# Three operand buffers declared further down in on-chip memory

## The chip, the cores and the metric

The kernel runs on one NeuronCore of a Trainium2 chip. The metric is the device time of one execution in microseconds (us). A core has a matmul engine (TensorE, PE in the profile, its weight loads shown apart as PEld), a vector engine (VectorE, DVE), an activation engine (ScalarE, ACT), GpSimd (POOL) and a queue that issues the DMAs (SyncE, SP). They share an on-chip memory (SBUF) of 128 partitions. A buffer has the same byte offset in each partition.

## The reference

A model of width 1024 on 256 tokens. Two layers of a transformer-like block come first:

```python
for i in range(DEPTH):                      # DEPTH = 2
    h = rmsnorm(x, norm1_g[i])
    mix = hybrid_mixer(h, w_in[i], ...)     # three kinds of sparse attention, 16 heads
    x = x + mix @ w_out[i]
    h = rmsnorm(x, norm2_g[i])
    x = x + conv_glu_ffn(h, w_up[i], conv_w[i], conv_b[i], w_down[i])   # hidden width 2816
return rmsnorm(x, final_g)
```

A third layer follows, with four branches of width 256 (a linear recurrence, pooling, a gated chunked recurrence, a short convolution), which are projected to 1024, gated, summed and sent through `w_out`; then a feed-forward block with hidden width 4096 and a squared ReLU:

```python
merged = jnp.sum(gates * branch_out, axis=2)
h = h + rms_norm(jnp.einsum("btd,de->bte", merged, w_out[l]), norm_mix_post[l])
hid = jnp.square(jax.nn.relu(jnp.einsum("btd,df->btf", rms_norm(h, ...), w_up[l])))
h = h + rms_norm(jnp.einsum("btf,fd->btd", hid, w_down[l]), norm_mlp_post[l])
```

All is fp32.

## The kernel before

**Weights.** `stream_plan` lists about 170 tiles of 128 x 2048 fp32 values in the order of use. SyncE loads them into the four slots of `raw`. ScalarE rounds a tile to fp32r into `whi` (L1288); VectorE (L1744) or GpSimd (L2575) subtracts and stores the rest into `wlo`. Both have three slots.

**Activations** are split in the same way into a high and a low part: `hh` and `hl`, the halves of `hb2`, for the input of a projection, `gh` and `gl` for the hidden values of a feed-forward block. A product is the sum of three fp32r matmuls: high x high, high x low, low x high.

**`gh`, `gl`, `mg`** hold [128, 2, 2, 256] fp32r values each, 4096 bytes per partition. They serve four ends:
- the hidden values between `up` and `down`: ScalarE writes `gh` (L1421, and L1718 in the third layer), VectorE `gl` (L2105, L2540), PE reads both in `down` (L720 to L722) and `down_quarter` (L734 to L736);
- the first two blocks of the attention's output (`mixed_at`) before `w_out`, read at L577, L578 and L580;
- the output of a branch of the third layer, read at L1211 to L1213;
- the merged branches (`merged_at`), `gh`, `gl` and `mg` before `w_out` of the third layer.

In all of these matmuls the piece of `gh`, `gl` or `mg` is the first operand, the one that is loaded into the array (LDWEIGHTS, 128 x 128), and 512 columns of `whi` or `wlo` stream through:

```python
ah, al = gh[:, j % 2, k, s], gl[:, j % 2, k, s]
...
e.matmul(o, ah, wh[:, k, c], start=j == 0 and k == 0, stop=False)
e.matmul(o, ah, wl[:, k, c], start=False, stop=False)
mm = e.matmul(o, al, wh[:, k, c], start=False, stop=last and k == 1)
```

In the `up` matmuls (L697, L702, L703) it is the other way: a weight slot is loaded, and `hb2` streams, 512 columns (high and low) or 256.

**Order.** Each engine's program is written out by hand, with semaphores between them. No planner decides anything by a buffer's address.

**Where buffers lie.** `sb` allocates in the order of the calls. Each start is rounded up to 32 bytes, and `raw` starts at byte 16,512. So the starts before are, in bytes per partition:

| buffer | start | | buffer | start |
|---|---|---|---|---|
| raw | 16,512 | | PQ | 150,176 |
| whi | 49,280 | | gb | 193,696 |
| wlo | 73,856 | | rl | 197,792 |
| X | 98,432 | | E | 201,888 |
| XN | 106,624 | | PT | 210,080 |
| hb2 | 114,816 | | sm | 214,176 |
| gh | 131,200 | | sc | 218,784 |
| gl | 135,296 | | selm | 220,832 |
| mg | 139,392 | | vbd | 221,856 |
| prmt | 143,488 | | cc | 223,136 |
| mskt | 147,872 | | th, lv | 225,184, 227,232 |

`prmt` has 4376 bytes, which isn't a multiple of 32. The buffers up to it start at multiples of 64, those behind it 32 bytes past a multiple of 64.

Of the kernel before, what the change touches and what calls it, by code (L numbers as in the profile page):

```python
# [8 lines left out]
F32R = mybir.dt.float32r  # L9
# [6 lines left out]
L = 256  # L16
# [128 lines left out]
def program(nc, wst, prm, msk, prm2, gains, lvl, x, out):  # L145
    ctx = ExitStack()
    with ctx:
        def sb(name, shape, dt=F32):
            return ctx.enter_context(nc.sbuf_tensor(name, shape, dt))
# [14 lines left out]
        XN = sb("XN", [128, 2, D])  # L164
        hb2 = sb("hb2", [128, 8, 2, L], F32R)
        hh, hl = hb2[:, :, 0, :], hb2[:, :, 1, :]
        gh = sb("gh", [128, 2, 2, L], F32R)
        gl = sb("gl", [128, 2, 2, L], F32R)
        mg = sb("mg", [128, 2, 2, L], F32R)
        prmt = sb("prmt", [128, NPRM])  # L170
        mskt = sb("mskt", [128, 9, 128], BF16)
        PQ = sb("PQ", [128, 2 * PCOLS + 22 * L])
# [7 lines left out]
        sc = sb("sc", [128, 2, L])  # L180
        selm = sb("selm", [128, 2, L], BF16)
        vbd = sb("vbd", [80, 5, 64])
        cc = sb("cc", [128, 2, L])
        th = sb("th", [128, 2, L])
        lv = sb("lv", [128, 8, 128], mybir.dt.uint16)
# [2665 lines left out]
```

How the kernel before makes its waits and increments, by code:

```python
    def wait_ge(self, sem, value):  # L129
        if self.seen.get(sem.name, 0) < value:
            self.e.wait_ge(sem, value)
            self.seen[sem.name] = value
# [374 lines left out]
        def rope(e, q, room, step, done, c0, nh, hd, r2, cos, sin):  # L507
            n = 2 * nh * r2
            view = P[:, :, c0:c0 + nh * hd].rearrange("p t (h d) -> p t h d", d=hd)
            x1, x2 = view[:, :, :, 0:r2], view[:, :, :, r2:2 * r2]
            tb = [w[:, 0:n].rearrange("p (t h r) -> p t h r", t=2, r=r2) for w in room]
            def tab(name):
                return par(name).rearrange("p (t r) -> p t r", t=2).unsqueeze(2).broadcast_to([128, 2, nh, r2])
            e.tensor_tensor(tb[0], x1, tab(cos), ALU.mult)
            e.tensor_tensor(tb[1], x2, tab(sin), ALU.mult)
            e.tensor_tensor(tb[2], x2, tab(cos), ALU.mult)
            e.tensor_tensor(tb[3], x1, tab(sin), ALU.mult).then_inc(*step())
            q.wait_ge(*q.prev)
            e.tensor_tensor(x1, tb[0], tb[1], ALU.subtract)
            e.tensor_tensor(x2, tb[2], tb[3], ALU.add).then_inc(*done)
# [6 lines left out]
            def bank_free(b):  # L529
                if free[b] is not None:
                    q.wait_ge(*free[b])
# [1 line left out]
            def weights_ready(m):  # L533
                q.wait_ge(*hi[m])
                q.wait_ge(*lo_of(m)[m])
# [1 line left out]
            def keep_warm(n, bank):  # L537
                q.wait_ge(*dve["warm"])
                bank_free(bank)
                for i in range(n):
```

## Time and profile before

| | |
|---|---|
| runs of the kernel before | 1032.85, 1035.64, 1035.68 us (median 1035.64) |
| the profiled execution's own time | 1032.85 us |
| its span, first to last instruction | 1031.5 us |
| PE busy | 1021.9 us, 99% |
| PE weight loads | 858.8 us, 83% |
| VectorE, ScalarE, GpSimd busy | 765.6, 551.4, 224.8 us |
| mean granted TensorE clock | 1.000 |
| DMA | 179.16 MB, 174 GB/s |

The profile is of one execution. Weight loads overlap the matmuls before them. Busy time of an engine is the union of its instructions; a wait is idle time of an engine, put down to what ended it. "Chain" is the sequence of work that ended last, followed backwards from the last instruction.

### The profile page before, as it was taken

To read this page: it belongs to the slowest core of one execution; us is meant where nothing else is said; L and a number is where in the kernel's file an instruction comes from. 1 tells how busy PE (TensorE), PEld (TensorE's weight loads), DVE (VectorE), ACT (ScalarE), POOL (GpSimd) and SP (SyncE) were. 2 spreads that over 40 slices of the span, in tenths; PEclk is the share of its full clock that TensorE was granted. 3 is DMA by queue.
4 is the path that set the end of the run, shared out by engine and by line. 5 is a ranking of instruction groups with operands and counts; after the bars stand their busy time and mean duration, and the time that the engine had idled before them with its cause. 6 is when DMAs were issued, how large, how long until landed. Compare 5 with 4: busy or idle time off the path is not lost.

```text
span 1031.5 us, 14779 instructions
## 1 busy us (share of the span) xinstructions
PE 1021.9 (99%) x5714; PEld 858.8 (83%) x5714; DVE 765.6 (74%) x1221; ACT 551.4 (53%) x831; POOL 224.8 (22%) x311
## 2 busy tenths in 40 slices
PE   8999999999999999999999999999999999999997
PEld 6877788888888877788888888998888878888886
DVE  6987678788777887578787778978855457666665
ACT  6575656555456466656455556755434545434432
POOL 0270600000000280600000003128967620000000
PEclk9999999999999999999999999999999999999999
DMA  9451455555554351365554554543535555555541
GB/s 360 152 201 46 146 181 183 190 189 205 193 184 174 117 210 42 123 222 193 204 204 166 202 186 164 175 172 105 180 124 196 212 184 223 176 207 191 178 149 41
DMA packets 26822, 179.16 MB, mean 174 GB/s; under 512 B 2944, under 2 KB 3072, under 8 KB 6272
## 3 DMA queue, kind: packets, MB, share of 16 engines
q1 hardware_dynamic: 26752, 178.22, 48.5%
q8 instruction: 45, 0.74, 0.3%
q14 instruction: 25, 0.20, 0.1%
HBM read 177.16 MB, written 1.05 MB: 173 GB/s over the span
## 4 chain that ended last, share of the span: by engine, by line
PE 98%; DVE 1%; ACT 1%; issue 0%; DVEq 0%; ACTq 0%
PE pb L697 17%; PE pb L702 10%; PE pb L577 9%; PE pb L578 9%; PE pb L580 8%; PE pb L720 6%; PE pb L722 6%; PE pb L721 6%; PE pb L703 2%; PE pb L958 2%; PE pb L914 2%; PE pb L623 1%; PE pb L622 1%; PE pb L624 1%; PE pb L1124 1%; PE pb L926 1%
## 5 line engine op out<-in xcount | busy, mean ns | idle before, releaser
L1744 DVE TENSOR_TENSOR wlo<-raw,whi 128x2048 fp32r<-128x2048 f32 x127 | 290.6, 2290 | 108.2 <-ACT whi L1288 108.0
L1288 ACT ACTIVATE whi<-raw 128x2048 fp32r<-128x2048 f32 (+1 forms) x164 | 304.9, 1863 | 62.3 <-PE pb L580 31.4
L2575 POOL TENSOR_TENSOR wlo<-raw,whi 128x256 fp32r<-128x256 f32 x260 | 197.6, 798 | 322.8 <-ACT whi L1288 322.6
L697 PE MATMUL pb<-hb,whi 128*128 128x512 f32 x770 | 194.0, 391 | 0.0
L697 PEld LDWEIGHTS pb<-hb,whi 128*128 128x128 f32 x770 | 144.9, 188 | 28.8
L577 PE MATMUL pb<-whi,hb 128*128 128x512 f32 x344 | 137.8, 401 | 0.0
L578 PE MATMUL pb<-wlo,hb 128*128 128x512 f32 x344 | 134.0, 390 | 0.0
L580 PE MATMUL pb<-whi,hb 128*128 128x512 f32 x328 | 128.0, 390 | 0.0
L702 PEld LDWEIGHTS pb<-hb,wlo 128*128 128x128 f32 x880 | 120.1, 190 | 8.6
L702 PE MATMUL pb<-hb,wlo 128*128 128x256 f32 x880 | 122.7, 282 | 0.0
L720 PE MATMUL pb<-whi,gh 128*128 128x512 f32 x280 | 109.3, 391 | 0.0
L722 PE MATMUL pb<-whi,gl 128*128 128x512 f32 x280 | 109.1, 390 | 0.0
L721 PE MATMUL pb<-wlo,gh 128*128 128x512 f32 x280 | 108.9, 389 | 0.0
L2584 POOL TENSOR_TENSOR sm<-sm 128x1 f32<-128x1 f32 x12 | 6.5, 553 | 422.9 <-DVE sm L1752 242.6
L577 PEld LDWEIGHTS pb<-whi,hb 128*128 128x128 f32 x344 | 64.6, 188 | 17.8 <-issue 5.0
L578 PEld LDWEIGHTS pb<-wlo,hb 128*128 128x128 f32 x344 | 64.7, 188 | 12.5
L580 PEld LDWEIGHTS pb<-whi,hb 128*128 128x128 f32 x328 | 61.6, 188 | 13.1
L722 PEld LDWEIGHTS pb<-whi,gl 128*128 128x128 f32 x280 | 52.6, 188 | 11.4
L721 PEld LDWEIGHTS pb<-wlo,gh 128*128 128x128 f32 x280 | 52.6, 188 | 11.1
L720 PEld LDWEIGHTS pb<-whi,gh 128*128 128x128 f32 x280 | 52.7, 188 | 9.6
L1421 ACT ACTIVATE gh<-th 128x512 fp32r<-128x512 f32 x22 | 13.9, 632 | 76.3 <-DVE th L2102 76.3
L703 PE MATMUL pb<-hb,whi 128*128 128x512 f32 x110 | 43.6, 396 | 0.0
(388 smaller groups left out, 1561.2 us busy)
## 6 DMA issues: line engine op xcount, KB each, us to landing
raw<-wst SPq DMA_DIRECT2D x160, 1024.0 KB, 4.8
raw<-wst SPq DMA_DIRECT2D x8, 512.0 KB, 3.6
gb<-gains SPq DMA_DIRECT2D x3, 512.0 KB, 5.7
X<-x SPq DMA_DIRECT2D x2, 512.0 KB, 5.7
out<-X SPq DMA_DIRECT2D x4, 256.0 KB, 2.1
PQ<-prm SPq DMA_DIRECT2D x1, 909.0 KB, 4.4
raw<-wst SPq DMA_DIRECT2D x2, 256.0 KB, 7.1
prmt<-prm SPq DMA_DIRECT2D x1, 479.0 KB, 10.1
```

The costliest lines, as they stand in the source:

```text
L577: e.matmul(o, high[:, s], wh[:, k, :], start=first and k == 0, stop=False)
L578: mm = e.matmul(o, high[:, s], wl[:, k, :], start=False, stop=False)
L580: mm = e.matmul(o, low[:, s], wh[:, k, :], start=False, stop=last and k == 3)
L697: e.matmul(both, wh[:, k, s], hb2[:, k, :, :].rearrange("p i q -> p (i q)"), start=k == 0, stop=False)
L702: e.matmul(high, wl[:, k, s], hh[:, k, :], start=False, stop=False)
L703: mm = e.matmul(both, wh[:, 7, s], hb2[:, 7, :, :].rearrange("p i q -> p (i q)"), start=False, stop=True)
L720: e.matmul(o, ah, wh[:, k, c], start=j == 0 and k == 0, stop=False)
L721: e.matmul(o, ah, wl[:, k, c], start=False, stop=False)
L722: mm = e.matmul(o, al, wh[:, k, c], start=False, stop=last and k == 1)
L1288: e.activation(whi[:, split_slot(m), 0:w], raw[:, m % RAW, 0:w], ACT.Copy).then_inc(*hi(m))
L1744: e.tensor_tensor(wlo[:, split_slot(m), 0:w], raw[:, m % RAW, 0:w], whi[:, split_slot(m), 0:w].bitcast(F32), ALU.subtract).then_inc(*lo_v(m))
L2575: g = e.tensor_tensor(wlo[:, split_slot(m), s], raw[:, m % RAW, s], whi[:, split_slot(m), s].bitcast(F32), ALU.subtract)
```

## The change

The declarations of `gh`, `gl` and `mg` go from behind `hb2` to behind `vbd`. Nothing else is touched. The three buffers then start at 210,848, 214,944 and 219,040, and the eleven buffers from `prmt` to `vbd` start 12,288 bytes lower than before; `cc`, `th` and `lv` stay.

```diff
         hb2 = sb("hb2", [128, 8, 2, L], F32R)
         hh, hl = hb2[:, :, 0, :], hb2[:, :, 1, :]
-        gh = sb("gh", [128, 2, 2, L], F32R)
-        gl = sb("gl", [128, 2, 2, L], F32R)
-        mg = sb("mg", [128, 2, 2, L], F32R)
         prmt = sb("prmt", [128, NPRM])
...
         vbd = sb("vbd", [80, 5, 64])
+        gh = sb("gh", [128, 2, 2, L], F32R)
+        gl = sb("gl", [128, 2, 2, L], F32R)
+        mg = sb("mg", [128, 2, 2, L], F32R)
         cc = sb("cc", [128, 2, L])
```

## Rows read from the trace of the kernel before

**Rows 1.** The page: span, and busy time, share and instructions of each engine.

```profile
span 1031.5 us, 14779 instructions
PE 1021.9 (99%) x5714; PEld 858.8 (83%) x5714; DVE 765.6 (74%) x1221; ACT 551.4 (53%) x831; POOL 224.8 (22%) x311
```

**Rows 2.** The page: the chain that ended last, by engine.

```profile
PE 98%; DVE 1%; ACT 1%; issue 0%; DVEq 0%; ACTq 0%
```

**Rows 3.** Waits of PE's matmuls: for whom, us, times, longest.

```profile
PE pb L599 <- ACT whi L1350: 1.5, 1, 1.5
PE pb L541 <- DVE sm L2556: 1.5, 1, 1.5
PE pb L681 <- DVE hb L1766: 0.8, 1, 0.8
PE pb L958 <- DVE XN L2192: 0.3, 2, 0.2
```

**Rows 4.** Windows: stretch, length, busy by engine (instructions), clock, DMA, GB/s.

```profile
140.00:312.00 172.00, 172.00 (x920) 148.74 (x919) 137.80 (x192) 94.84 (x122) 0.43 (x1) 1.00 0.56 195
455.00:625.00 170.00, 170.00 (x908) 146.94 (x907) 134.60 (x165) 92.00 (x118) 0.00 (x0) 1.00 0.55 194
```

**Rows 5.** Tiles gh and mg: ns min/median/max, first and last start.

```profile
L720 PEld LDWEIGHTS pb<-whi,gh x280: 186/188/192, 159.6 to 1019.6; 128*128 128x128 f32 x140
L577 PEld LDWEIGHTS pb<-whi,gh x40: 186/188/190, 106.1 to 831.7; 128*128 128x128 f32 x40
L1211 PEld LDWEIGHTS pb<-whi,gh x32: 187/188/192, 722.7 to 821.2; 128*128 128x128 f32 x32
L734 PEld LDWEIGHTS pb<-whi,gh x24: 186/188/190, 314.5 to 1025.1; 128*128 128x128 f32 x24
L577 PEld LDWEIGHTS pb<-whi,mg x8: 187/188/188, 823.3 to 833.0; 128*128 128x128 f32 x8
```

**Rows 6.** Timeline of PEld in `down`: start, us; first and last of 11.

```profile
473.97 0.19 PEld L720 LDWEIGHTS pb<-whi,gh 128*128 128x128 f32 x1
...
476.24 0.19 PEld L721 LDWEIGHTS pb<-wlo,gh 128*128 128x128 f32 x1
```

**Rows 7.** Timeline of PEld, six loads for 256-column matmuls, merged.

```profile
158.70 0.79 PEld L702 LDWEIGHTS pb<-hb,wlo 128*128 128x128 f32 x6
```

**Rows 8.** Line 1124: its weight loads, and eight of them in the timeline.

```profile
L1124 PEld LDWEIGHTS pb<-PQ,rl x32: 186/188/193, 699.4 to 752.3; 128*128 128x128 f32 x32
L1124 PEld LDWEIGHTS pb<-gb,rl x24: 187/190/193, 706.6 to 742.3; 128*128 128x128 f32 x24
706.59 1.72 PEld L1124 LDWEIGHTS pb<-gb,rl 128*128 128x128 f32 x8
```

**Rows 9.** Timeline of PEld over the loads of mg; first and seventh.

```profile
823.28 0.19 PEld L577 LDWEIGHTS pb<-whi,mg 128*128 128x128 f32 x1
...
824.64 0.19 PEld L577 LDWEIGHTS pb<-whi,gh 128*128 128x128 f32 x1
```

**Rows 10.** Groups by form: busy us, mean ns, idle before and its releaser.

```profile
L2105 DVE TENSOR_TENSOR gl<-th,gh 128x512 fp32r<-128x512 f32 x22 | 15.2, 692 | 15.4 <-ACT gh L1421 15.4
L2083 DVE TENSOR_TENSOR E<-E,rl 128x512 f32<-128x512 f32 x22 | 15.2, 692 | 0.7
L1421 ACT ACTIVATE gh<-th 128x512 fp32r<-128x512 f32 x22 | 13.9, 632 | 76.3 <-DVE th L2102 76.3
L1417 ACT ACTIVATE th<-cc 128x512 f32<-128x512 f32 x22 | 13.8, 625 | 8.4 <-DVE cc L2093 8.4
L1298 ACT ACTIVATE XN<-X 128x512 f32<-128x512 f32 x20 | 12.5, 637 | 6.4 <-DVE X L1794 3.5 <-DVE X L1787 2.9
```

**Rows 11.** Timelines of DVE and PEld in the first feed-forward stage.

```profile
155.40 0.69 DVE L2105 TENSOR_TENSOR gl<-th,gh 128x512 fp32r<-128x512 f32 x1 [0.70 <-ACT gh L1421]
...
159.57 0.19 PEld L720 LDWEIGHTS pb<-whi,gh 128*128 128x128 f32 x1
```

## The prediction

> **What bounds the kernel now.** I read the page's engine line first [rows 1]: TensorE (PE) is busy for 1021.9 of 1031.5 us, at the full granted clock in all 40 slices, VectorE for 74% and ScalarE for 53%. The chain that ended last [rows 2] says the same in another way: 98% of it is PE, 1% VectorE, 1% ScalarE. The waits of PE [rows 3] come to 1.5 + 1.5 + 0.8 + 0.3 = 4.1 us in the whole program, none of them on a buffer that the change names. The windows [rows 4] show the two long feed-forward stages, where `gh` and `gl` do most of their work: PE is busy for 172.00 of 172.00 us, while VectorE has 34 us and ScalarE 77 us to spare. The kernel is a stream of matmuls with no holes, so the time moves only if the distance between matmuls moves, or if another engine becomes so late that a hole opens.
>
> **What the change does, part by part.** No instruction, wait, semaphore or DMA is added, removed or reordered. Only addresses change. From the sizes in the code, each start rounded up to 32 bytes: `gh`, `gl` and `mg` (4096 bytes per partition each) leave 131,200, 135,296 and 139,392 and go to 210,848, 214,944 and 219,040, between `vbd` and `cc`. The eleven buffers `prmt` to `vbd` move down by 12,288 bytes, which is 3 x 4096, so their places within 64, 256 or 4096 bytes stay as they were. `raw`, `whi`, `wlo`, `X`, `XN`, `hb2`, `cc`, `th` and `lv` stay. One thing does change about alignment: 131,200 is a multiple of 64, and 210,848 is 32 past one. No DMA reads or writes the three buffers.
>
> **Part 1, the matmuls that load `gh`, `gl` or `mg`.** Their count from the tile rows [rows 5]: L720 to L722 280 each, L577, L578 and L580 40 each with `gh` or `gl` and 8 each with `mg`, L1211 to L1213 32 each, L734 to L736 24 each. That is 3 x (280 + 40 + 8 + 32 + 24) = 1152 of 5714. In each of them the 128x128 piece of `gh`, `gl` or `mg` is the weight load and `whi` or `wlo` streams.
> The load takes 188 ns at the median, wherever it comes from. The distance from one to the next is (476.24 - 473.97) / 10 = 0.227 us for `gh` and `gl` [rows 6] and (824.64 - 823.28) / 6 = 0.227 us for `mg` [rows 9]. A load of 188 ns is thus hidden under a period of 227 ns, with 39 ns to spare.
> Does a start 32 bytes past a multiple of 64 cost anything? The kernel before has such operands already: in L1124 both inputs (`rl`, `E`, `gb` or `PQ`) lie in buffers that start 32 past a multiple of 64. Their loads take 187/190/193 and 186/188/193 ns [rows 8], against 186/188/192 for `gh`. They are plain fp32 matmuls, not fp32r, so the row is near but not the same thing. Its loads follow each other at (1.72 - 0.19) / 7 = 0.219 us, also well above the load. Bounds for one matmul: below, 0; above, 193 - 188 = 5 ns, if the slowest load of that row were typical and nothing hid it, which is 1152 x 0.005 = 5.8 us. I take 0, because the medians are equal within 2 ns and 39 ns of cover lie over them. The term is 0.0 us.
> A gain must be bounded too. The period has a fixed part. 256-column matmuls (L702) follow each other at (0.79 - 0.19) / 5 = 0.120 us [rows 7], 512-column ones at 0.227: 256 columns more cost 107 ns, so 512 cost 213 or 214 ns and 13 ns belong to no column. Were this part a clash over where the two operands lie, and gone with the new address, it would be 1152 x 0.013 = 15.0 us. But it is the same 13 ns with `gh` at 131,200, with `mg` at 139,392, and (L702) with a weight slot as the load and `hb2` streaming; nothing in it follows the address. I take 0.
> The Trainium skill ("TensorE: Matmul & The Clock Gate", section "Back-to-back issue gap") gives an isolated gap of N/2.4 + 2.5 ns, 216 ns for 512 columns, 11 ns less than the 227 of these rows. By the page's figure, if the missing 11 ns hung on the operands' place, the sum would be an estimated 1152 x 0.011 = 12.7 us lower; that would speak for the rival of the gain below. No run here shows such a gap yet.
>
> **Part 2, the instructions that write the three buffers.** ScalarE writes `gh` from `th` in 632 ns; `th` from `cc` takes 625 and `XN` from `X` 637 [rows 10]. VectorE writes `gl` in 692 ns and `E` from `E` and `rl`, all three 32 past a multiple of 64, in 692 [rows 10]. Aligned or not, the same shape costs the same. If they cost 7 ns more each, cover is there: in the first feed-forward stage `gl` is ready at 155.40 + 0.69 = 156.09, and the first load that needs it or its partner starts at 159.57 [rows 11], 3.5 us later. Nothing queued behind them on VectorE or ScalarE is on PE's path, since PE doesn't wait in this stage [rows 4]. Term: 0.0 us. Without that cover it would be 7 ns on each of the 22 + 22 writes of these rows, 0.3 us.
>
> **Part 3, the eleven buffers that slide.** They are read and written by VectorE, ScalarE, GpSimd, PE and a few DMAs. Their alignment is unchanged, so only a cost that hangs on the absolute place could appear. On the chain these two engines have 2% of the span, 21 us [rows 2]; even 5% more on each of those instructions is 1.0 us. In the feed-forward stages 34 us of VectorE's idle time would have to be filled first. I take 0, with 0 to 1.0 us as bounds.
>
> **Sum.** 1032.85 us of the profiled execution (span 1031.5 and 1.35 around it) + 0.0 + 0.0 + 0.0 = 1032.85. That execution is the fastest of the three shown; the others took 1035.64 and 1035.68. With a difference of nothing the median stays the median: 1035.6 us. The spread of these runs is 2.8 us, 0.27%, so 0.3% (3.1 us) is about what a measurement can tell from no change.
>
> **The rivals.**
> Slower: the load of a piece that starts 32 bytes past a multiple of 64 takes longer as fp32r than the fp32 rows show, or its period does. With 5 ns exposed on each of 1152 matmuls the time is 1035.6 + 5.8 = 1041.4. It decides from 3.1 / 1152 = 2.7 ns on each. For it: no row before has an fp32r load at such an address. Against: 39 ns of cover, and L1124. Chance 0.06.
> Faster: part of the 13 ns between matmuls is a clash between load and stream that the new distance (from 131,200 to 210,848, with `whi` and `wlo` at 49,280 to 98,432) avoids. In full: 1035.6 - 15.0 = 1020.6. Against: three different pairs of places show the same 13 ns. Chance 0.04.
> The slide costs or gives something on VectorE, ScalarE or GpSimd, whose instructions are not tied to a period as PE's are. The bound is 1.0 us either way, so it ends as no change; a part of it that reached 3.1 us would need 15% on everything of the chain that isn't PE. Chance 0.05 as a cause that can be seen in the trace, 0.02 of it past 0.3%, equally to both sides.
> The change does nothing that the clock sees: my forecast, and with the slide's share within the bound 0.88 for a time within 0.3%.
>
> **How the numbers follow.** The likeliest case gives 1035.6. Its own spread is that of the runs, whose fastest is 1032.85, widened by the 0.3% above: 1032.0 to 1039.0. This holds 0.88 less a little for a median at the edge, so more than 8 in 10, and the rivals at 1020.6 and 1041.4 stay outside. Faster: 0.04 + 0.01, and 0.01 for the spread, 0.06. Slower: 0.06 + 0.01 less the part of that rival under 2.7 ns, 0.06. Within 0.3%: 0.88.
>
> **What would show it.** Right: L720's load at 188 and its period at 0.227 us as before, `gh` and `gl` writes at 632 and 692 ns, PE 172.00 of 172.00 us in the same window, PE's waits near 4 us. The slower rival would show as a longer LDWEIGHTS or a period of 0.230 us and more at L720 to L722 alone, with L697 (`hb2`, not moved) unchanged. The faster one would show periods nearer to 0.214 us there. The slide would show as a change of VectorE's or ScalarE's mean in groups on `PQ`, `E` or `PT`. The prediction is wrong if the address alone changes how a read of SBUF is served, which the trace before can show only for the places that it uses.

## The result, and the profile after

The changed kernel takes 1039.57 us (median of 5 runs, 1039.45 to 1042.50), the kernel before 1033.16 us (5 runs, 1032.69 to 1035.68). The ratio is 1.0061, with a 95% interval of 1.0047 to 1.0076: slower by 0.6%, some 6.3 us. Executions of most kernels here fall at two levels some 3 us apart, and both of these medians are of the lower one. The prediction had said 1035.6, no change, with a range that ended at 1039.0.

The page of the changed kernel gives the span, the engines and the chain, as [rows 1] and [rows 2] do for the kernel before:

```profile
span 1038.1 us, 14777 instructions
PE 1027.8 (99%) x5712; PEld 858.0 (83%) x5714; DVE 766.0 (74%) x1221; ACT 551.6 (53%) x831; POOL 224.5 (22%) x311
PE 98%; DMA 1%; DVE 1%; ACT 0%; issue 0%; SPq 0%; DVEq 0%
```

The span grew by 6.6 us and PE's busy time by 5.9. Weight loads, VectorE, ScalarE and GpSimd are where they were, within 1 us. The waits of PE are those of [rows 3], the first 0.3 us longer, and one of 0.4 us on a DMA at the start:

```profile
PE pb L599 <- ACT whi L1350: 1.8, 1, 1.8
PE pb L541 <- DVE sm L2556: 1.5, 1, 1.5
PE pb L681 <- DVE hb L1766: 0.8, 1, 0.8
PE pb L554 <- DMA X<-x: 0.4, 1, 0.4
PE pb L958 <- DVE XN L2192: 0.3, 2, 0.2
```

So no hole opened. The same two windows as in [rows 4]:

```profile
140.00:312.00 172.00, 172.00 (x915) 147.60 (x914) 137.13 (x189) 94.47 (x123) 0.56 (x2) 1.00 0.55 191
455.00:625.00 170.00, 170.00 (x904) 145.88 (x903) 133.38 (x161) 92.29 (x117) 0.00 (x0) 1.00 0.56 193
```

PE is still busy for all of 172.00 and 170.00 us, but gets through 915 and 904 matmuls there instead of 920 and 908. Each takes longer. The tile `gh` (ns min/median/max, first and last start) shows where, and what not:

```profile
L720 PEld LDWEIGHTS pb<-whi,gh x280: 186/188/192, 159.7 to 1026.1; 128*128 128x128 f32 x140
L720 PE MATMUL pb<-whi,gh x280: 392/395/396, 159.9 to 1026.3; 128*128 128x512 f32 x140
L577 PEld LDWEIGHTS pb<-whi,gh x40: 186/188/190, 106.1 to 835.8; 128*128 128x128 f32 x40
L1421 ACT ACTIVATE gh<-th x22: 631/632/633, 154.9 to 627.9; 128x512 fp32r<-128x512 f32 x22
```

The weight load takes 188 ns as in [rows 5], and ScalarE's write 632 as in [rows 10]. The matmul's median went from 389 to 395 ns; the same row and two others of the kernel before, for this and for the experiments:

```profile
L720 PE MATMUL pb<-whi,gh x280: 389/389/398, 159.8 to 1019.9; 128*128 128x512 f32 x140
L697 PE MATMUL pb<-hb,whi x770: 389/389/398, 148.6 to 1013.7; 128*128 128x512 f32 x193
L577 PE MATMUL pb<-whi,hb x344: 389/389/583, 13.1 to 844.1; 128*128 128x512 f32 x172
```

The first load of L720 starts 0.1 us later than before (159.6 in [rows 5]), the last 6.5 us later (1019.6): the whole loss builds up between them. Where it builds up can be seen in the timeline of weight loads, which has `down` tiles of 24 matmuls between `up` tiles. First the kernel before:

```profile
485.04 1.58 PEld L697 LDWEIGHTS pb<-hb,whi 128*128 128x128 f32 x7
...
487.84 0.19 PEld L720 LDWEIGHTS pb<-whi,gh 128*128 128x128 f32 x1
...
489.00 0.19 PEld L722 LDWEIGHTS pb<-whi,gl 128*128 128x128 f32 x1
...
493.30 1.55 PEld L697 LDWEIGHTS pb<-hb,whi 128*128 128x128 f32 x7
```

Then the changed kernel:

```profile
489.79 0.19 PEld L720 LDWEIGHTS pb<-whi,gh 128*128 128x128 f32 x1
...
490.95 0.19 PEld L722 LDWEIGHTS pb<-whi,gl 128*128 128x128 f32 x1
...
495.38 1.57 PEld L697 LDWEIGHTS pb<-hb,whi 128*128 128x128 f32 x7
```

A tile's first five distances between loads come to 1.16 us in both kernels, 0.232 each. They come behind the 256-column matmuls of an `up` tile (L702) and one of L703. The other 19 take 4.30 us before, 0.226 each, and 4.43 after, 0.233 each. So the kernel before also has the slow period at first and then settles at the short one; the changed kernel never settles, although every load is as short as before and PE waits for nobody.

The tile as a whole takes 493.30 - 487.84 = 5.46 us before and 5.59 after, 5 ns more for each matmul. 1152 matmuls times 5 ns is 5.8 us. Most of the rest is in L697, which the change doesn't touch: its seven loads behind a `down` tile take 1.57 us, not 1.55, and its busy time on the two pages went from 194.0 to 194.7 us:

```profile
L697 PE MATMUL pb<-hb,whi 128*128 128x512 f32 x770 | 194.0, 391 | 0.0
L697 PE MATMUL pb<-hb,whi 128*128 128x512 f32 x770 | 194.7, 392 | 0.0
```

The experiments below are compared by one number: the time from the first load of this `down` tile, the second of its layer, to the first load of the `up` tile behind it. The starts are rounded to 0.01 us, so a difference of two can be off by as much. The tile is typical: 33 of the 35 `down` tiles take 5.47 or 5.48 us in the trace before and 33 take 5.59 us after. The first tile of each of the first two feed-forward stages is an exception (5.43 us before, 5.56 and 5.57 after). Where an unused buffer is declared ahead, these lines are one or two numbers later.

### The profile page after: what moved, and what is told of

The parts are those of the page before. It is cut to its first block, busy times and chain, and to the rows that moved or that the text cites. A ratio compares the mean times of both kernels' runs of the same rounds, so it can differ in the third digit from the quotient of the medians.

```text
span 1038.1 us, 14777 instructions
## 1 busy us (share of the span) xinstructions
PE 1027.8 (99%) x5712; PEld 858.0 (83%) x5714; DVE 766.0 (74%) x1221; ACT 551.6 (53%) x831; POOL 224.5 (22%) x311
## 4 chain that ended last, share of the span: by engine, by line
PE 98%; DMA 1%; DVE 1%; ACT 0%; issue 0%; SPq 0%; DVEq 0%
PE pb L697 17%; PE pb L702 10%; PE pb L577 9%; PE pb L578 9%; PE pb L580 8%; PE pb L722 6%; PE pb L721 6%; PE pb L720 6%; PE pb L703 2%; PE pb L958 2%; PE pb L914 2%; PE pb L623 1%; PE pb L624 1%; PE pb L622 1%; PE pb L1124 1%; PE pb L926 1%
## 5 line engine op out<-in xcount | busy, mean ns | idle before, releaser
L697 PE MATMUL pb<-hb,whi 128*128 128x512 f32 x770 | 194.7, 392 | 0.0
L697 PEld LDWEIGHTS pb<-hb,whi 128*128 128x128 f32 x770 | 144.9, 188 | 29.8
L577 PE MATMUL pb<-whi,hb 128*128 128x512 f32 x344 | 137.9, 401 | 0.0
L580 PE MATMUL pb<-whi,hb 128*128 128x512 f32 x328 | 128.1, 391 | 0.0
L702 PEld LDWEIGHTS pb<-hb,wlo 128*128 128x128 f32 x880 | 120.1, 190 | 8.7
L702 PE MATMUL pb<-hb,wlo 128*128 128x256 f32 x880 | 122.7, 282 | 0.0
L722 PE MATMUL pb<-whi,gl 128*128 128x512 f32 x280 | 110.9, 396 | 0.0
L720 PE MATMUL pb<-whi,gh 128*128 128x512 f32 x280 | 110.6, 395 | 0.0
L721 PE MATMUL pb<-wlo,gh 128*128 128x512 f32 x280 | 110.5, 395 | 0.0
L577 PEld LDWEIGHTS pb<-whi,hb 128*128 128x128 f32 x344 | 64.6, 188 | 17.9 <-issue 5.0
L580 PEld LDWEIGHTS pb<-whi,hb 128*128 128x128 f32 x328 | 61.6, 188 | 13.2
L722 PEld LDWEIGHTS pb<-whi,gl 128*128 128x128 f32 x280 | 52.6, 188 | 12.6
L721 PEld LDWEIGHTS pb<-wlo,gh 128*128 128x128 f32 x280 | 52.6, 188 | 12.5
L720 PEld LDWEIGHTS pb<-whi,gh 128*128 128x128 f32 x280 | 52.7, 188 | 11.0
L703 PE MATMUL pb<-hb,whi 128*128 128x512 f32 x110 | 43.5, 395 | 0.0
```

The source lines that it names most:

```text
L577: e.matmul(o, high[:, s], wh[:, k, :], start=first and k == 0, stop=False)
L580: mm = e.matmul(o, low[:, s], wh[:, k, :], start=False, stop=last and k == 3)
L697: e.matmul(both, wh[:, k, s], hb2[:, k, :, :].rearrange("p i q -> p (i q)"), start=k == 0, stop=False)
L702: e.matmul(high, wl[:, k, s], hh[:, k, :], start=False, stop=False)
L703: mm = e.matmul(both, wh[:, 7, s], hb2[:, 7, :, :].rearrange("p i q -> p (i q)"), start=False, stop=True)
```

## The experiments

"Distance" is the difference of two buffers' starts by 256 bytes. That this is the right number is what the experiments found; some expectations still think in 64 or 512. In the kernel before, `raw`, `whi`, `wlo`, `hb2`, `gh`, `gl` and `mg` all leave a remainder of 128 by 256, so all distances are 0. In the changed kernel `gh` to `mg` leave 160: a distance of 32. `whi`, `wlo`, `hb2`, `gh`, `gl` and `mg` are the split buffers; those at a distance of 0 from each other are called in step.

**1. Align them to 64 where they are now (low_aligned).**

```diff
+        sb("pad0", [128, 8])
         gh = sb("gh", [128, 2, 2, L], F32R)
```

> The changed kernel with 32 unused bytes declared in front of gh: gh, gl and mg lie at 210,880, 214,976 and 219,072, multiples of 64, 32 bytes from where the changed kernel has them; cc, th and lv move 32 bytes up as well. Theory (alignment): a loaded piece that starts 32 past a multiple of 64 costs about 6.7 ns more per matmul, so here the period of L720 to L722 returns to 0.227 us and the time to the kernel before's, 1033 to 1036 us. Rival (place): the lower place, or its distance from the weight slots, costs it, so the period stays at 0.233 us and the time at 1039 to 1040 us.

1040.69 us (6 runs), ratio 1.0062 (1.0044 to 1.0080). Nothing is gained, and the tile takes 498.17 - 492.58 = 5.59 us. The theory that the new start's being 32 past a multiple of 64 costs, the one with which the slower rival had been priced, has fallen: 210,880 is a multiple of 64. The distance is now 64.

**2. Leave them in their old place, 32 bytes off (high_off32).**

```diff
+        sb("pad0", [128, 8])
         gh = sb("gh", [128, 2, 2, L], F32R)
         gl = sb("gl", [128, 2, 2, L], F32R)
         mg = sb("mg", [128, 2, 2, L], F32R)
+        sb("pad1", [128, 8])
```

> The kernel before with 32 unused bytes in front of gh and 32 behind mg: gh, gl and mg stay in their place but start 32 past a multiple of 64 (131,232, 135,328, 139,424); all buffers behind keep their remainder by 64. Alignment theory: 1152 matmuls x 6.7 ns = 7.7 us at most, as measured 6.4, so 1039 to 1041 us, period 0.233 us. Place rival: no change, 1033 to 1036 us, period 0.227 us.

1040.67 us (6 runs), ratio 1.0065 (1.0050 to 1.0081). The whole loss comes back without the move, from 32 bytes, and the tile takes 498.83 - 493.24 = 5.59 us. So the low place isn't needed for it, and, with run 1, neither is a start off a multiple of 64.

**3. Align the buffers behind `prmt` to 64 (all_aligned).**

```diff
         prmt = sb("prmt", [128, NPRM])
+        sb("pad0", [128, 8])
         mskt = sb("mskt", [128, 9, 128], BF16)
```

> The kernel before with 32 unused bytes between prmt and mskt: PQ, gb, rl, E, PT, sm and all behind now start at multiples of 64. Alignment theory, if it holds for plain fp32 loads as for fp32r: the matmuls that load from PQ, E, PT, rl (some 1000) get up to 6.7 ns shorter each, up to 6 us faster, 1027 to 1032 us. Rival: only loads that are followed by 512 streamed columns of fp32r show the cost, the fp32 ones are bound by their own passes; no change, 1033 to 1036 us, L1124's loads still 0.219 us apart.

1033.17 us (12 runs), ratio 0.9998 (0.9987 to 1.0010): no change. The plain fp32 matmuls don't care: the eight loads of L1124 (one line later here) take 1.71 us where [rows 8] has 1.72.

```profile
706.63 1.71 PEld L1125 LDWEIGHTS pb<-gb,rl 128*128 128x128 f32 x8
```

**4. Put `hb2` off instead (hb2_off32).**

```diff
+        sb("pad0", [128, 8])
         hb2 = sb("hb2", [128, 8, 2, L], F32R)
...
+        sb("pad1", [128, 8])
         gh = sb("gh", [128, 2, 2, L], F32R)
```

> The kernel before with 32 unused bytes in front of hb2 and 32 behind it: hb2 alone starts 32 past a multiple of 64. It is loaded at L577, L578 and L580 (1016 matmuls) and streamed at L697, L702, L703, L622 to L624, L659 to L664 and L681 (about 2400). If only the load suffers: 1016 x 6.7 ns = 6.8 us slower, 1040 to 1042 us, L577 to L580 at 0.233 us and L697 still at 0.227. If streaming suffers too: L697 and L702 grow as well, 10 to 25 us slower. Place rival: no change.

1044.70 us (4 runs), ratio 1.0101 (1.0085 to 1.0118). The expectation took `gh` as unmoved; in fact the two unused buffers put it 64 bytes off, so L720 to L722 were hit as well as L577 to L580: 1016 + 1152 = 2168 matmuls. The loss, 11.2 us over this batch's 1033.5, can't be shared among these alone, for it also hurts when `hb2` streams (lines are two later):

```profile
L699 PE MATMUL pb<-hb,whi x770: 390/394/397, 150.2 to 1025.4; 128*128 128x512 f32 x193
L579 PE MATMUL pb<-whi,hb x344: 392/396/587, 13.0 to 853.5; 128*128 128x512 f32 x172
```

Both medians were 389 before. Matmuls with 256 streamed columns got a little faster. Here are one group of them before and the same group in this run, then the group of L702 in this run (busy us, mean ns, idle before), which has a mean of 279 ns against 282 on the page of the kernel before:

```profile
L623 PE MATMUL pb<-hb,whi x120: 280/283/283, 648.5 to 693.0; 128*128 128x256 f32 x120
L625 PE MATMUL pb<-hb,whi x120: 277/278/282, 655.5 to 698.9; 128*128 128x256 f32 x120
L704 PE MATMUL pb<-hb,wlo 128*128 128x256 f32 x880 | 120.7, 279 | 0.0
```

**5. Shift everything by 32 (all_shift32).**

```diff
+        sb("pad0", [128, 8])
         raw = sb("raw", [128, RAW, CH])
```

> The kernel before with 32 unused bytes in front of raw, so that raw, whi, wlo, hb2, gh, gl and mg all start 32 bytes later; what a matmul loads and what it streams keep their distance. Absolute theory (any loaded or streamed piece off a multiple of 128 costs): all 512-column matmuls slow down, some 3300 x 6.7 ns = 22 us, 1055 us. Relative theory (only the difference between the loaded and the streamed piece's starts counts): no change, 1032 to 1036 us, L720 and L697 at 0.227 us.

1033.37 us (11 runs), ratio 0.9999 (0.9988 to 1.0009). All split buffers now start 32 past a multiple of 64, and nothing is lost. This run decides between an operand's own alignment and the distance between operands. Its tile takes 496.49 - 491.02 = 5.47 us, as before:

```profile
491.02 0.19 PEld L721 LDWEIGHTS pb<-whi,gh 128*128 128x128 f32 x1
...
496.49 1.55 PEld L698 LDWEIGHTS pb<-hb,whi 128*128 128x128 f32 x7
```

**6. Far away, same remainder (far_same_phase).** `gh`, `gl`, `mg`, then `prmt` and `mskt`, are declared behind `selm`. Against the kernel before:

```diff
-        gh = sb("gh", [128, 2, 2, L], F32R)
-        gl = sb("gl", [128, 2, 2, L], F32R)
-        mg = sb("mg", [128, 2, 2, L], F32R)
-        prmt = sb("prmt", [128, NPRM])
-        mskt = sb("mskt", [128, 9, 128], BF16)
...
         selm = sb("selm", [128, 2, L], BF16)
+        gh = sb("gh", [128, 2, 2, L], F32R)
+        gl = sb("gl", [128, 2, 2, L], F32R)
+        mg = sb("mg", [128, 2, 2, L], F32R)
+        prmt = sb("prmt", [128, NPRM])
+        mskt = sb("mskt", [128, 9, 128], BF16)
         vbd = sb("vbd", [80, 5, 64])
```

> gh, gl and mg behind selm, at 202,880, 206,976 and 211,072, 71,680 bytes higher than before but the same remainder by 512 (128) as whi, wlo and hb2; prmt, mskt and vbd follow them, PQ to selm slide down by 16,672. Remainder theory, absolute or relative: 1032 to 1036 us, period 0.227. Place rival (high addresses cost): 1039 to 1041 us, period 0.233.

1032.93 us (11 runs), ratio 0.9994 (0.9982 to 1.0006). 71,680 bytes further away cost nothing.

**7 and 8. Small distances.** One buffer `gg` holds all three, as views that start later. The edit for 8, 16 and 96 bytes (`sm`, a scratch buffer, gives back the room):

```diff
-        gh = sb("gh", [128, 2, 2, L], F32R)
+        gg = sb("gg", [128, 3096], F32R)
+        gh = gg[:, 2:1026].rearrange("p (i k q) -> p i k q", i=2, k=2)
+        gl = gg[:, 1028:2052].rearrange("p (i k q) -> p i k q", i=2, k=2)
+        mg = gg[:, 2072:3096].rearrange("p (i k q) -> p i k q", i=2, k=2)
```

> The kernel before with the three buffers in their place, gh 8 bytes, gl 16 bytes and mg 96 bytes later relative to a multiple of 128. Relative theory: each offset shows its own period at the lines that load it (gh: L720, L721; gl: L722; mg: L577 to L580 near 830 us). If the step is at 32-byte or 64-byte boundaries, 8 and 16 cost nothing (0.227) and 96 costs 0.233; if any offset costs, all three show 0.233; time 1032 to 1041 us.

> As before with gh 64, gl 128 and mg 192 bytes later. If a remainder by 128 decides, gl's loads (L722) stay at 0.227 us while gh's and mg's take 0.233; if a remainder by 512 (the size of one piece) decides, all three take 0.233. Absolute or relative alike; time 1037 to 1041 us.

One run each: 1040.01 us, inside what was expected, and 1036.74 us, just below it. Single runs say little on the size. The tiles say more: 497.31 - 491.77 = 5.54 us with `gh` 8 and `gl` 16 bytes off, and 494.80 - 489.26 = 5.54 us with 64 and 128. Even 8 and 16 bytes cost more than half of what 32 do.

```profile
491.77 0.19 PEld L721 LDWEIGHTS pb<-whi,gg 128*128 128x128 f32 x1
...
497.31 1.58 PEld L698 LDWEIGHTS pb<-hb,whi 128*128 128x128 f32 x7
```

No offset showed a period of its own. With 64 and 128 bytes the medians over the trace are 229 ns from L720 to L721, 236 from L721 to L722 and 228 from L722 to the next L720 (numbered one higher there). The middle one is the distance behind a load of `gh` with `wlo` streaming. All three at 64 (run 1) or all at 128 (run 15) cost more, 5.59 and 5.58 us a tile, so the loss isn't a sum over single buffers.

**9. Weights and `gh` shifted together, `hb2` not (weights_gh_shift32).**

```diff
         raw = sb("raw", [128, RAW, CH])
+        hb2 = sb("hb2", [128, 8, 2, L], F32R)
+        hh, hl = hb2[:, :, 0, :], hb2[:, :, 1, :]
+        sb("pad0", [128, 8])
         whi = sb("whi", [128, SPL, CH], F32R)
...
-        hb2 = sb("hb2", [128, 8, 2, L], F32R)
-        hh, hl = hb2[:, :, 0, :], hb2[:, :, 1, :]
```

> hb2 declared ahead of whi, and 32 unused bytes between them: hb2 keeps its remainder by 512 (128), whi, wlo, gh, gl and mg all have 160. Relative theory: what is loaded from gh or gl against a streamed whi or wlo keeps its distance, so L720 to L722 stay at 0.227 us, while loads from hb2 against whi and wlo (L577 to L580) take 0.233 and L697 0.233 to 0.234; time 4 to 7 us over before, 1037 to 1041 us. Absolute rival (a remainder other than 128 costs whatever the other operand is): L720 to L722 at 0.233 as well, 1045 us and more. Theory of the place or order of buffers: no rule, any value.

1041.26 us (4 runs), ratio 1.0072 (1.0057 to 1.0087), 0.3 us past the range expected. Within one kernel both halves of the theory can be seen (tile `whi`, lines one later):

```profile
L698 PE MATMUL pb<-hb,whi x770: 392/395/397, 151.3 to 1022.3; 128*128 128x512 f32 x193
L578 PE MATMUL pb<-whi,hb x344: 392/396/587, 12.7 to 852.0; 128*128 128x512 f32 x172
L721 PE MATMUL pb<-whi,gh x280: 389/389/396, 162.6 to 1028.4; 128*128 128x512 f32 x140
```

`gh` at a remainder of 160 is at 389 ns here, since `whi` and `wlo` have 160 too, and the `down` tile takes 5.45 us. `hb2` at its old remainder of 128 is at 395 and 396, since it alone kept it.

**10 to 12. Only `wlo` off (wlo_plus32, wlo_plus64, wlo_minus32).** `wlo` is declared behind `mg`, with 32 or 64 unused bytes ahead, or behind `prmt` with 192 (for `wlo_minus32`, which also takes 128 bytes from `sm`). The edit for 32:

```diff
-        wlo = sb("wlo", [128, SPL, CH], F32R)
...
         mg = sb("mg", [128, 2, 2, L], F32R)
+        sb("pad0", [128, 8])
+        wlo = sb("wlo", [128, SPL, CH], F32R)
```

> wlo alone 32 bytes off the other split buffers (declared behind mg, 32 unused bytes ahead of it). wlo is streamed in some 730 matmuls (L578, L721, L1212, L735) and loaded in some 1240 with 256 streamed columns (L702, L624). From the run with hb2 moved: 512 columns at a distance of 32 cost about 6 ns, 256 columns gain about 2 to 5 ns. So +730 x 6 = +4.4 us and -1240 x 2 to 5 = -2.5 to -6 us: -2 to +2 us against before, 1031 to 1037. Rival (only the loaded buffer's own address matters): +1240 x 5 = 6 us, 1040.

> As the run before with 64 bytes. If 64 costs less than 32 for 512 columns (the scan of gh gave 231 against 233 ns) and gains as much for 256, 730 x 4.5 = +3.3 us and -1240 x 2 to 5: -3 to +1 us, 1030 to 1036.

> wlo at remainder 96, that is 32 bytes below the other split buffers (prmt declared ahead of it and the scratch buffer sm cut to the 1120 columns that are used). If the sign of the distance doesn't matter: as with plus 32. If it does, this is the run that has the loaded wlo at the distance at which the run with hb2 moved had its gain for 256 columns (loaded start minus streamed start = -32): L702 at 0.117 us and below; 1029 to 1037 us.

1041.74, 1040.44 and 1041.07 us (4 runs each), ratios 1.0081 (1.0066 to 1.0096), 1.0066 (1.0049 to 1.0082) and 1.0076 (1.0060 to 1.0092). All three expectations missed: I had added a cost for each matmul with `wlo` as stream and a gain for each with `wlo` as load, and hoped for a kernel faster than both. The gain was small: L702 has a mean of 281, 281 and 279 ns against 282. The tile shows the larger error. Only 8 of its 24 matmuls stream `wlo`, yet with 32 bytes it takes 497.36 - 491.79 = 5.57 us (and 5.57 and 5.60 in the other two), nearly as much as with `gh` and `gl` off:

```profile
491.79 0.19 PEld L721 LDWEIGHTS pb<-whi,gh 128*128 128x128 f32 x1
...
497.36 1.55 PEld L698 LDWEIGHTS pb<-hb,whi 128*128 128x128 f32 x7
```

**13. Keep the change, move `prmt` behind the three (after_prmt_behind).** Against the changed kernel:

```diff
-        prmt = sb("prmt", [128, NPRM])
...
         mg = sb("mg", [128, 2, 2, L], F32R)
+        prmt = sb("prmt", [128, NPRM])
         cc = sb("cc", [128, 2, L])
```

> The changed kernel with one more line moved: prmt is declared behind mg. So gh, gl and mg lie at 206,464, 210,560 and 214,656, as low in the list as in the changed kernel, but with the remainder 128 by 512 that whi, wlo and hb2 have. Remainder theory: the change's cost is gone, 1032 to 1036 us, down's period 0.227 us. Rival (the low place itself costs): 1039 to 1041 us.

1033.08 us (11 runs), ratio 0.9995 (0.9983 to 1.0008). This is the changed kernel without its loss. `gh` lies at 206,464; 206,464 and 49,280 (`whi`) have the same remainder by 256. The only thing wrong with the change was that `prmt`, 4376 bytes, came ahead of `gh` and gave the 32 bytes. The tile takes 496.41 - 490.95 = 5.46 us:

```profile
490.95 0.19 PEld L720 LDWEIGHTS pb<-whi,gh 128*128 128x128 f32 x1
...
496.41 1.55 PEld L697 LDWEIGHTS pb<-hb,whi 128*128 128x128 f32 x7
```

**14 and 15. By which power of two? (high_plus256, high_plus128).** `vbd`, 1280 bytes, or 128 unused bytes (taken from `sm`) are declared ahead of `gh`. The edit for 256:

```diff
         hh, hl = hb2[:, :, 0, :], hb2[:, :, 1, :]
+        vbd = sb("vbd", [80, 5, 64])
         gh = sb("gh", [128, 2, 2, L], F32R)
...
-        vbd = sb("vbd", [80, 5, 64])
```

> vbd (1280 bytes) declared ahead of gh, so that gh, gl and mg start 256 bytes off the others by 512, in their old neighbourhood. If the remainder by 512 decides: period 0.231 to 0.233 us, 1037 to 1041 us. If the remainder by 256 or 128 decides: 0.227 us, 1032 to 1036 us.

> 128 unused bytes ahead of gh (the scratch buffer sm is cut to the 1120 columns that are used). If the remainder by 128 decides: period 0.227 us, 1032 to 1036 us. If that by 512 (or 256): 0.231 to 0.233 us, 1037 to 1041 us.

256 off: 1033.46 us (10 runs), ratio 1.0001 (0.9989 to 1.0013), no change. 128 off: 1039.54 us (4 runs), ratio 1.0055 (1.0035 to 1.0076). So buffers 256 apart are in step, and buffers 128 apart are not. The tiles, first with 256 and then with 128:

```profile
487.68 0.19 PEld L720 LDWEIGHTS pb<-whi,gh 128*128 128x128 f32 x1
...
493.15 1.55 PEld L697 LDWEIGHTS pb<-hb,whi 128*128 128x128 f32 x7
```

```profile
489.83 0.19 PEld L721 LDWEIGHTS pb<-whi,gh 128*128 128x128 f32 x1
...
495.41 1.58 PEld L698 LDWEIGHTS pb<-hb,whi 128*128 128x128 f32 x7
```

They take 5.47 and 5.58 us.

**16. Only `gl` off (only_gl_off32).**

```diff
         gh = sb("gh", [128, 2, 2, L], F32R)
-        gl = sb("gl", [128, 2, 2, L], F32R)
         mg = sb("mg", [128, 2, 2, L], F32R)
+        sb("pad0", [128, 8])
+        gl = sb("gl", [128, 2, 2, L], F32R)
+        sb("pad1", [128, 8])
```

> Only gl starts 32 bytes off the others; gh, mg, whi, wlo and hb2 stay congruent. One load in three of down is off. If each load pays for itself: one interval of three is 0.233 us, the mean 0.229, and the cost a third, about 2.1 us, 1034 to 1037 us. If one operand out of step slows its neighbours too, as with wlo off: the mean is 0.232 us and the cost most of the whole, 1038 to 1041 us.

1042.07 us (4 runs, 1039.32 to 1042.85), ratio 1.0069 (1.0048 to 1.0090). One load in three is off, and the cost isn't a third but the whole. Its tile takes 495.80 - 490.20 = 5.60 us. As in runs 10 to 12, one operand out of step slows the matmuls beside it: the medians over the trace are 229 ns from L720 to L721, 233 from L721 to L722 and 239 from L722 (the load of `gl`) to the next L720, where the kernel before has 227 three times.

```profile
490.20 0.19 PEld L722 LDWEIGHTS pb<-whi,gh 128*128 128x128 f32 x1
...
495.80 1.56 PEld L699 LDWEIGHTS pb<-hb,whi 128*128 128x128 f32 x7
```

**Together.** The kernels with all split buffers in step by 256 (3, 5, 6, 13, 14) lie within 0.06% of the kernel before, whatever their place. All others that ran more than once lose 0.55% to 1.0%. None was faster than the kernel before beyond the noise.

The tile sorts them in the same way, as the median over the 35 `down` tiles of each trace:

| what is out of step, and by how many bytes | kernels | `down` tile, us |
|---|---|---|
| nothing | before, 3, 5, 6, 13, 14 | 5.47 |
| `hb2` alone, which the tile doesn't use | 9 | 5.45 |
| `gh` 8 and `gl` 16; `gh` 64 and `gl` 128 | 7; 8 | 5.54 |
| `wlo` 32; 64 | 10; 11 | 5.57 |
| `gh` and `gl` 128 | 15 | 5.58 |
| `gh` and `gl` 32; 64 | changed, 2; 1 | 5.59 |
| `wlo` 32 the other way; `gl` alone 32; `hb2` 32 with `gh` and `gl` 64 | 12; 16; 4 | 5.60 |

## Why the prediction was wrong

- **What bounds the kernel** held: PE's stream without holes, so that only the distance between matmuls can move the time. It did, by 5 ns on 1152 of them, 5.8 of the 6.6 us that the span grew.
- **Part 1 failed, at the sentence "nothing in it follows the address. I take 0."** The reason given was that the period's fixed 13 ns were the same with `gh` at 131,200, with `mg` at 139,392 and with a weight slot as the load. These are not three kinds of place. `raw` starts at 16,512, and every buffer up to `mg` has a size that is a multiple of 4096, so all of these starts leave 128 by 256. And the 13 ns were worked out from L702 and a 512-column period together, so L702 couldn't confirm them. Samples of one case were taken for three cases. The trace before held no fp32r matmul with its operands out of step; what was unknown should have been weighed as unknown. In place of nothing the runs showed 5 ns on each of the 1152 (5.47 to 5.59 us a tile), and the start by 256 as what decides (runs 2, 5, 13 and 14).
- **The trace before already had two periods**, which the prediction didn't look for. Seven loads of L697 take 1.58 us behind 256-column matmuls and 1.55 behind a `down` tile, which is 1.39 / 6 = 0.232 and 1.36 / 6 = 0.227 us each, with the same buffers. So part of the period depends on what ran just before, and a fixed 13 ns wasn't a sound reading. It would have shown that some 5 ns can come and go without a longer load.
- **The question was asked of one operand.** Whether a start 32 past a multiple of 64 costs something was tested on L1124, and rightly answered with no (runs 1, 3 and 5 agree). The sum needed another question: how does the new start stand to that of the buffer that streams? The prediction noted the remainders by 256 for the buffers that slide, and not for the three that move.
- **The 39 ns of cover** said that a longer load would be hidden. No load got longer. The distance between matmuls grew instead, where this cover doesn't help.
- **The slower rival** is what happened by its sign, place and size: 1041.4 forecast, 1039.57 measured, 5.8 us priced from the 5 ns bound against some 6.3, shown at L720 to L722 as a period above 0.230 with the load unchanged. L697 was to stay as it was, and didn't quite: it is slower behind each `down` tile. Its stated cause, the start's own remainder by 64, is refuted by run 1. The 5 ns were the slowest load of another kind of matmul, and no load got slower, so that they met the measured 5 ns is luck. Its chance of 0.06 was too small, and the range ended below it.
- **The faster rival**, that a different distance takes away part of the 13 ns: none of the sixteen runs did this for 512 columns. With 256 columns there is a gain of that kind, 283 to 278 ns for L623 in run 4, too small to pay for the rest. The Trainium skill's 216 ns for 512 columns ("TensorE: Matmul & The Clock Gate", "Back-to-back issue gap") isn't reached in any of them; the shortest steady period is 0.227 us, so whether the other 11 ns hang on places stays open.
- **The sum** started from 1035.6 us, 2.4 above the 1033.16 that five runs gave. So the time missed by 4.0 us, and the term that had been put at nothing by 6.4.
- **Parts 2 and 3** held. Writes took 632 and 693 ns, against 632 and 692, and run 3 moved the slid buffers' alignment at no cost.
- The Trainium skill ("SBUF — State Buffer", section "Who interferes with whom") gives PE two independent read ports, one for the stream and one for the weight load, and says that PE never waits on anyone. No run here shows a wait of PE on another engine's reads. But where PE's own two operands lie to each other changed the period from 0.227 to 0.233 us, so the places of the two matter to each other, whatever the cause, and here the measurement decides.

**What stays open.** The runs show the rule and not the mechanism. Why 256 bytes is the step (one run, 14, stands for it against 512), why 8 and 16 bytes cost 5.54 us a tile and 32 cost 5.59, why one operand in three slows all, and why the stream starts slow behind 256-column matmuls even in step, wasn't settled. A clash of PE's two reads in the same part of the memory would fit, and is only argued.

## What to carry to other kernels

Where fp32r matmuls of 512 columns run back to back, let the starts of everything that is loaded and everything that is streamed agree by 256 bytes; one odd-sized buffer declared ahead of one of them is enough to lose it. Here that was worth 0.6%. When a trace says that addresses don't matter, first write down the addresses it has seen, by every power of two. A period that is equal in a few groups of a trace shows only that these groups are alike; look at the groups where it differs, too.

## What was not expected of the hardware

- A buffer's offset of 8 to 128 bytes against the others, within 256, costs 0.07 to 0.13 us per 24 matmuls, without any longer load, wait or lower clock; 256 and 71,680 bytes cost nothing.
- With everything in step, a stream of 512-column matmuls behind 256-column ones still starts with distances of 0.232 us and settles at 0.227 (the `down` tile before: 1.16 us for five distances, then 4.30 for nineteen). The seven L697 loads of an `up` tile behind such matmuls take 1.58 us, those behind a `down` tile 1.55.
- With 256 streamed columns being out of step costs nothing and gains a little (mean of L702 282 before, 279 in run 4). Plain fp32 (L1124) shows no difference, 1.72 and 1.71 us.
